# A chunked recurrence on one core: the next block's preparation spread differently over the inversion's levels

## What is computed

```python
r, k, v, w_lo, a_lo = split(zf)                  # zf: the shifted and mixed input
kk = to_heads(k * rw_kk);  kk = kk / max(sqrt(sum(kk * kk)), 1e-12)
for d in range(2):                               # forward and backward in time
    w = -softplus(-(w0[d] + tanh(w_lo) @ w2[d])) - 0.5
    decay = exp(-exp(w))
    a = sigmoid(a0[d] + a_lo @ a2[d])
    kd = kh * (1.0 + (a - 1.0) * k_a)
    y, s = wkv7_scan(rh, decay, kd, vh, -kk, kk * a, s0[d], reverse=(d == 1))
        # S = S * w_t + (S a_t) b_t^T + v_t k_t^T ;  y_t = S r_t
    bonus[d] = sum(rh * kd * r_k) * vh
```

## Time and profile before

| | us |
|---|---|
| median of three runs | 2466.56 (2465.54 to 2466.6) |
| the profiled execution | 2462.29 |
| its span | 2460.6 |
| TensorE busy in the span | 2263.6 (92%) |
| VectorE, ScalarE, GpSimd busy | 1551.8, 1009.5, 265.3 |
| steady part of the recurrence, 1500 to 1600 us: TensorE busy | 91.04 |

### The profile page before, as it was taken

How to read it: one execution, slowest core, us unless ns; L and a number is a source line. 1 busy time by engine, 2 the same in 40 slices (tenths; PEclk the granted TensorE clock), 3 DMA queues, 4 the chain that set the end, 5 groups by cost and what they waited for, 6 DMA issues and landing times. The chain is left out here.

```text
span 2460.6 us, 66375 instructions
## 1 busy us (share of the span) xinstructions
PE 2263.6 (92%) x26630; PEld 1853.4 (75%) x26630; DVE 1551.8 (63%) x2611; ACT 1009.5 (41%) x1734; POOL 265.3 (11%) x335
## 2 busy tenths in 40 slices
PE   4999999999899999999947899999788799899998
PEld 2788878888688887888836777777657576688887
DVE  5756566666865456665635777777456676856754
ACT  5444234544532123445424555555333666411111
POOL 0000000000000000000031222222124663000000
PEclk7999999999999999999978999999978899999999
DMA  7344333333242333333330111110068523834542
GB/s 240 107 135 125 111 94 111 113 117 102 94 129 93 96 108 97 106 111 119 107 101 25 32 41 32 32 56 17 19 214 305 126 94 95 288 115 171 197 152 88
DMA packets 250306, 277.75 MB, mean 113 GB/s; under 512 B 30683, under 2 KB 174171, under 8 KB 247643
## 3 DMA queue, kind: packets, MB, share of 16 engines
q1 hardware_dynamic: 245306, 266.95, 33.9%
q10 hardware_dynamic: 4576, 8.40, 0.9%
q0 software_dynamic: 320, 0.98, 0.2%
HBM read 184.66 MB, written 91.62 MB: 112 GB/s over the span
## 5 line engine op out<-in xcount | busy, mean ns | idle before, releaser
L715 PE MATMUL proj_ps<-h_hi,w_hi 128*128 128x512 f32 x1656 | 649.5, 392 | 27.6 <-DVE h_lo L465 19.7
L716 PE MATMUL proj_ps<-h_lo,w_hi 128*128 128x512 f32 x1656 | 647.0, 391 | 0.0
L717 PE MATMUL proj_ps<-h_hi,w_lo 128*128 128x512 f32 x1656 | 646.4, 390 | 0.0
L318 ACT CAST w_hi<-w_raw 128x512 fp32r<-128x512 f32 x420 | 255.1, 621 | 694.0 <-PE proj_ps L717 353.2
L715 PEld LDWEIGHTS proj_ps<-h_hi,w_hi 128*128 128x128 f32 x1656 | 312.3, 189 | 98.2 <-issue 26.1
L717 PEld LDWEIGHTS proj_ps<-h_hi,w_lo 128*128 128x128 f32 x1656 | 312.2, 189 | 65.6
L716 PEld LDWEIGHTS proj_ps<-h_lo,w_hi 128*128 128x128 f32 x1656 | 312.4, 189 | 62.9
L482 DVE TENSOR_TENSOR w_lo<-w_raw,w_hi 128x512 fp32r<-128x512 f32 x420 | 283.2, 689 | 44.3 <-ACT w_hi L318 43.7
L498 DVE TENSOR_TENSOR z_slots<-proj_ps,x_rows 128x512 f32<-128x512 f32 x174 | 120.2, 691 | 169.9 <-PE proj_ps L717 167.9
L498 DVE TENSOR_TENSOR x_rows<-proj_ps,x_rows 128x512 f32<-128x512 f32 x116 | 80.1, 691 | 108.9 <-PE proj_ps L717 102.9
L1010 POOL MEMSET rpb_padded<- 60x127 f32 x1 | 0.2, 198 | 1261.3 <-POOLq L89 1261.3
(11 more groups left out here) (380 smaller groups left out, 4101.4 us busy)
## 6 DMA issues: line engine op xcount, KB each, us to landing
w_raw<-in_w_in SPq DMA_DIRECT2D x240, 256.0 KB, 3.0
scratch_gatesT<-z_slots SPq DMA_DIRECT2D x128, 256.0 KB, 2.7
late_rows<-scratch_gatesT SPq DMA_DIRECT2D x64, 512.0 KB, 4.4
scratch_zT<-z_slots SPq DMA_DIRECT2D x108, 256.0 KB, 2.4
ada<-in_ada_w SPq DMA_DIRECT2D x4, 2048.0 KB, 15.2
late_rows<-scratch_zT SPq DMA_DIRECT2D x4, 2048.0 KB, 12.7
late_rows<-scratch_branchT SPq DMA_DIRECT2D x16, 512.0 KB, 5.3
late_rows<-in_x SPq DMA_DIRECT2D x16, 512.0 KB, 4.9
```

The lines of the kernel that those rows point to most:

```text
L318: A.copy(wh[:, i, :, :], raw[:, q, :, :]).then_inc(w_hi, 1)
L715: T.matmul(out, wh[:, i, k, :], hi[:, o, k, :], start=(first and k == 0), stop=False, skip_group_check=not first)
L716: T.matmul(out, wh[:, i, k, :], lo[:, o, k, :], start=False, stop=False, skip_group_check=not first)
L717: last = T.matmul(out, wl[:, i, k, :], hi[:, o, k, :], start=False, stop=(k == 3), skip_group_check=not first)
```

## The change

No product and no activation is removed; they change places, and one pair changes engine.

- TensorE: the key sums go from level 4 to level 3, and the turn of K from level 3 to level 4. The wait for the norm squares (their bank is written by the X product) goes to level 3 with them. The bonus product goes behind W. The A product at level 4 now waits for the K rows' copy, and the first scores wait for K, now the last of the hats.
- VectorE: `norms` is cut into the squares (ahead of `decay` at level 3), Newton's steps (behind `decay`, ahead of the level-4 mask) and the rows (level 4). The query hat goes to level 4 in d=1 units, kk_a to level 3 in d=0 units, and B is made ahead of K. A now waits until the present unit's A product has read its predecessor.
- ScalarE: `exps` is cut into `exp_up` and `exp_down`; both go ahead of the K rows' copy in d=1 units, in d=0 units `exp_up` alone, and `exp_down` ahead of the copy At.
- GpSimd: `key_rates` runs there as two TENSOR_SCALAR instructions behind the lora copy.

```diff
-                       + ["kd", "kds", "bt", "kk", "R", "kka", "A", "K", "B", "bonus"], U,
-                       leaves_out=(("Lx", "inc", "kds", "bt", "bonus"), block_v))
+        prep_v = Turns(ctx, nc, "prep_vector", [f"mix{j}" for j in mixes] + ["ksq", "nx", "lw", "L", "Lx", "inc"] + newton + ["kka1", "rx", "kd"]
+                       + ["kds", "bt", "R", "kk", "kka0", "A", "B", "K", "bonus"], U,
...
+            def key_rates(n, d):
+                prep_a.after(pool, (n, d), "ta1")
+                pool.sem_inc(pool_go, 1)
+                for m in range(2):
+                    last = nc.gpsimd.tensor_scalar(uu[:, m, :], aa[:, m, :], hka[:, m:m + 1], oka[:, m:m + 1], ALU.mult, ALU.add)
+                prep_g.done(last, d, "u")
...
             def rates(n, d):
-                prep_a.after(dve, (n, d), "u1")
+                prep_g.after(dve, (n, d), "u")
...
+            def key_rate_hat(n, d):
+                prep_a.after(dve, (n, d), "ta1")
+                prep_v.done(V.scalar_tensor_tensor(kka[:], aa[:], 1.0, kk[:], ALU.add, ALU.mult), d, f"kka{d}")
+
+            def query_hat(n, d):
+                prep_a.after(dve, (n, d), "EI")
...
             def hats(n, d):
...
+                    main_p.after(dve, (n, d), "A.", back=1)
                 done(V.scalar_tensor_tensor(chunks(AR[:, 0, :, :]), chunks(kk[:]), -1.0, padded(d, d), ALU.mult, ALU.mult), "A")
+                prep_v.after(dve, (n, d), f"kka{d}")
+                prep_a.after(dve, (n, d), "EN")
+                done(V.scalar_tensor_tensor(Bh[:], kka[:], 0.5, EN[:], ALU.mult, ALU.mult), "B")
                 prep_v.after(dve, (n, d), "kd")
                 done(V.tensor_tensor(Kh[:], kd[:, d], EN[:], ALU.mult), "K")
...
             def first_scores(u, back):
-                prep_v.after(pe, u, "B", back)
+                prep_v.after(pe, u, "K", back)
...
                     if v == 4:
-                        main_a.after(pe, u, "V.")
+                        main_a.after(pe, u, "Kt.")
...
-                    if v == 4 and more:
+                    if v == 3 and more:
                         prep_v.after(pe, u, "nx", -1)
```

More of the change, by code:

```diff
@@ L1113, in decay, with norm_squares @@
                     own(V.tensor_tensor(chunks(inc[:]), end, chunks(Lx[:]), ALU.subtract), "inc")
+            def norm_squares(n):
+                prep_p.after(dve, (n, 0), "ks")
+                prep_v.done(V.tensor_scalar(nx[:], ps[:, 4, 0:8], 1e-24, None, ALU.max), 0, "nx")
             def norms(n):
@@ L1234, in unit @@
                             bonus_rows(n)
+                        else:
+                            query_hat(*nxt)
                 if nxt:
@@ L1300, in rate, with exp_up, exp_down @@
                                 d, f"{name}{m}")
-            def key_rates(n, d):
-                prep_a.after(act, (n, d), "ta1")
-                for m in range(2):
-                    prep_a.done(A.activation(uu[:, m, :], aa[:, m, :], ACT.Identity, scale=hka[:, m:m + 1], bias=oka[:, m:m + 1]), d, f"u{m}")
-            def exps(n, d):
+            def exp_up(n, d):
+                prep_v.after(act, (n, d), "inc" if d else "L")
+                prep_a.done(A.activation(padded(d, 1 - d), chunks((inc if d else L)[:]), ACT.Exp, scale=0.5 * DECAY), d, "EI")
+            def exp_down(n, d):
                 own = lambda ins, name: prep_a.done(ins, d, name)
-                prep_v.after(act, (n, d), "inc" if d else "L")
-                run = chunks((inc if d else L)[:])
-                own(A.activation(padded(d, 1 - d), run, ACT.Exp, scale=0.5 * DECAY), "EI")
                 own(A.activation(EN[:], (inc if d else L)[:], ACT.Exp, scale=-0.5 * DECAY), "EN")
@@ L1357, in unit @@
                 factor(Z[:], "Z3.", 0)
-                rows(Kt, "Kt.", "K.")
                 if d == 0:
@@ L1540, in unit @@
                     between(v)
-                if more:
-                    prep_v.after(pe, u, "bt", -1)
-                    go()
-                    prep_p.done(mm(ps[:, 6, :], J[:], flat(kds[:])), 0, "bonus")
                 main_a.after(pe, u, "Z5.")
@@ L1551, in unit @@
                 if more:
+                    prep_v.after(pe, u, "bt", -1)
+                    go()
+                    prep_p.done(mm(ps[:, 6, :], J[:], flat(kds[:])), 0, "bonus")
                     first_scores(u, -1)
```

64 lines of the change are left out of this document (39 added, 25 removed).

## The result

| | before | after |
|---|---|---|
| median of 4 runs, us | 2466.05 (2462.32 to 2466.6) | 2481.09 (2480.41 to 2482.42) |
| ratio, 95% interval | 1 | 1.0062 [1.0048, 1.0075] |
| profiled execution: time, span, mean granted clock | 2462.29, 2460.6, 0.969 | 2481.74, 2480.0, 0.965 |

A forecast was written before the change was run, and what follows sets the result against it. TensorE was taken to set the pace (busy 91 of 100 us in the recurrence stage). 9 x 0.76 for d=0, 8 x (0.57 + 0.54) for d=1 and 0.4 gave +16 us on the median 2466.56: 2483 us, range 2475 to 2494.

The forecast's parts named there:

- Part 1: Bonus product behind W: the 0.86 us wait for b_hat goes, an equal one before W appears; gain 0.08 a unit.
- Parts 2 to 4: Levels 3 and 4, norm squares, Newton's steps and hats in d=1 units: first scores 0.57 us later a unit.
- Parts 2 and 5: Level 4 and ScalarE's exponential ahead of At in d=0 units: first scores 0.76 us later a unit.
- Part 6: Key rates on GpSimd: the first rate holds VectorE, costing 0.54 us a d=1 unit and 0 in d=0.
- Rival (a): GpSimd's key rates never hold VectorE, only the schedule costs: 11.8 us, so 2478; chance 0.30 together with (d).
- rival (b): GpSimd holds VectorE for the whole of both key rates, 0.81 us each: 26.1 us, so 2493; chance 0.21.
- (c): Faster: level 4 is on time, so d=1 units gain 0.74 us and d=0 units 0.08: 2460; chance 0.04.
- (d): The copy At does not hold the turned norms in d=0: 9 x 0.50 less, 2478; chance 0.30 with (a).
- (e): K_hat late again behind later turned norms: 0.5 us more a d=1 unit, 2487; chance 0.40 with the forecast.
- First block: Preparation of the first block, where the scan now stands behind the squares: 0.4 us more, between 0 and 1.7.

The follow-up runs named there:

- e7: The kernel before with only the hats and exponentials earlier (a variant of the change's part), bonus product still ahead of W: 2453.04 us, ratio 0.9958.
- e2: The changed kernel with the key rates back on ScalarE, right behind a_tanh: 2482.76 us, ratio 1.0063 to before.
- e11: The kernel before with only the key rates moved to GpSimd, behind its copy of the low-rank rows: 2465.48 us, ratio 0.9995.
- e3: The changed kernel with the downward exponential and the totals behind the copy At again in d=0 units: 2479.72 us, ratio 1.0049 to before.
- e5: The changed kernel with K turned at level 3 again and key sums, squares, Newton steps and norm rows at level 4: 2480.56 us, ratio 1.0060 to before.
- e10: The kernel before with only the levels moved (key sums at 3, K turned at 4), Newton's steps still behind the level-4 mask: 2477.06 us, ratio 1.0053.
- e4: The changed kernel with Newton's steps behind the level-4 mask instead of ahead of it in d=1 units: 2485.53 us, ratio 1.0081 to before.
- e12: The changed kernel with bonus product ahead of W, key rates on ScalarE and d=0 falling exponential behind the key-hat copy again: 2477.96 us, ratio 1.0042 to before.

## Why the prediction was right

Its value and sign held; its terms, one by one:

- **Part 1** held. Alone, the exchange moved the units by -0.00 and -0.04 (predicted -0.08), and the waits are the ones it named. What it lacked is the value of the old wait: it took the 0.86 as a full 0.86, and the W copies make it 0.41 (e7). That didn't enter its sum, since both sides of the exchange ended at the same place.
- **Parts 2 to 4**, d=1: predicted 0.57; with the rates on ScalarE, 27.41 - 26.82 = 0.59. X3's wait came as 0.35 for 0.5 (it starts 0.14 behind the squares' end, where the earlier trace rows have 0.24), level 4's gap as 1.38 within "1 to 2.3".
- **Parts 2 and 5**, d=0: predicted 0.76, measured 0.82, with 0.51 of it from the exponential.
- **Part 6** is the term whose mechanism failed: predicted 0.54 a d=1 unit, measured 0.28, in d=0 0.02 at most. The step that failed is that each rate would hold a chain without slack for its whole length. One rate did take 0.54 (between the 0.40 and 0.81 of its bounds), but log_w, which ran beside the first one, took 0.43 for 0.42, and the scan began 0.53 behind it, 0.52 before. The second rate stood still while the scan ran (1.12 each instead of 0.54). What VectorE lost is 0.08 on the scan and 0.18 on the first Newton step. Over the stage the term was 2.2 us instead of 4.3. Rival (a) falls by the unit lengths and durations of e2, not by its time; rival (b) falls by size. The Trainium skill, page "SBUF — State Buffer", section "SBUF: two separate sides", gives the shared ports to whichever of the two engines starts first, for a whole instruction (on VectorE's side one in a two-port mode or, against a GpSimd instruction that reads SBUF, one with two SBUF inputs). These rows agree in both directions: in e11 the copy lasts to 0.2 us behind the scan's end (1459.32 against 1459.12), in after the Newton step of 1467.54 ends where the rates end (1467.89 and 1467.86). Log_w beside the first rate shows no such hold.
- **Rivals (c) to (e)**: (c) falls with the gaps of 0.28 and 1.38 at level 4, (d) with e3, and (e) as the first scores of a d=1 unit wait for no hat.
- **First block**: predicted 0.4 (to 1.7), measured 3.0, outside its bounds. From the key sums to the first unit's first product it is 1310.41 - 1295.54 = 14.87 before and 1314.72 - 1296.87 = 17.85 after. VectorE before and after:

```profile
1300.54 0.43 DVE L1125 COPY kk_norm_rows<-kk_norm_inv 128x512 f32<-128x512 f32 x1 [0.86 <-DVE kk_norm_inv L1124]
```
```profile
1298.77 0.17 DVE L1127 TENSOR_SCALAR kk_norm_sq<-rw_ps 128x8 f32<-128x8 f32 x1 [20.42 <-PE rw_ps L1420]
1298.85 0.57 DVE L1118 TENSOR_SCALAR log_w<-log_w 128x512 f32<-128x512 f32 x1
1299.53 1.23 DVE L1119 TENSOR_TENSOR_SCAN log_run<-scan_keep,log_w 128x512 f32<-128x512 f32 x1
...
1305.33 0.43 DVE L1139 COPY kk_norm_rows<-kk_norm_inv 128x512 f32<-128x512 f32 x1 [2.50 <-issue]
```

  The decay rows, done long before the squares in the old order, now stand between the squares and Newton (+1.8); an idle piece behind the last Newton step grew from 0.86 to 2.50 (+1.6, named "issue", its cause open; in e5, with the old order here, a piece of 2.73 stands ahead of the last Newton step); the shorter tail of hats gives 0.5 back.

**The sum again, with what was measured:** waits of the units 9 x 0.82 + 8 x 0.59 = 12.1, the port 8 x 0.28 = 2.2, the first block 3.0: 17.3. The six stretches at half the clock, 1.54 in each of four d=0 units and less in two others, add about 7 in the profiled execution, 24 together. The first product of the following stage comes 24.7 later (1817.1 against 1792.4): 1.3 of it is there before the key sums (the projection, which the change leaves alone, ends later), 3.0 is the first block, 1.0 the first unit, 19.6 the fifteen units behind it, and the last two units give 0.2 back.

The end comes 19.4 later: from that product to the end before took 668.2 and after 662.9, and I leave those 5 us open. The medians are only 15.0 apart, since the profiled execution of before lay 3.8 under its median and that of after 0.7 over. So the forecast of 16 met 15 because two things that it didn't have, the clock (about 7) and more of the first block (+2.6), stand against three others: the port, which it had too large (-2.1), the 5 us that the rest of the program gave back, and the 4.4 between executions and medians. The waits of the units are shown part by part, in the lengths of one profiled execution each; that the total met the forecast to 2 us is largely luck.

## What to carry to other kernels

A wait in front of an instruction is worth only what it exceeds the next chain behind it: undo one cause and look which copy, mask or hat ends next, as the copies of W did behind b_hat. Work moved forward in a queue has to pass some product's mask; name the mask it now stands in front of (level 4 or level 5 here) before counting the gain at its old place. Try the parts of an edit one by one: the early hats alone, in the form of e7, were worth -0.4%, the levels alone +0.5%, and all together cost 0.6%.

## What the runs showed of the hardware

- A change of order that costs TensorE 0.3 us a unit can cost more than that again through its clock (e10: 5 us by waits, 7.5 by the clock). In seven kernels with the key sums at the third level the granted clock fell to 0.50 in 2 to 15 places of the stage, for 3.4 us each (once 6.8, in the first unit of e4); in six of the seven others, before among them, it did so at most once, and in the seventh, e5, five times. One costs up to 1.5 us in a steady unit.
- The place is nearly always the same. Of the 44 stretches in those seven kernels 41 begin behind the key sums (1.0 to 2.3 us from their start) and ahead of the V rows, where TensorE's idle pieces are no longer than 0.35; two lie in a first unit and one, in e4, behind the gap of 1.42 ahead of Z5. The five of e5 all stand behind such a gap (1.39 to 1.43). But not every unit of the same order has one, and in e12 the same kernel's runs differ by 22 us. What decides in which unit it happens stays open; I tried no kernel for that alone.
- VectorE and GpSimd hold each other in both directions: a GpSimd copy of 0.40 took 1.38 beside a scan, and a VectorE instruction of 0.17 took 0.35, one of 0.68 took 1.09 beside GpSimd. Not every VectorE instruction was held (log_w: 0.43 for 0.42 beside a rate), and where VectorE had an idle piece the same GpSimd work cost nothing.
